# Token blocks of 128 at the joins of a two-layer model's linears, one unit a weight load, six split slots

## The chip, the cores and the metric

The kernel runs on one core of a Trainium2 chip. The metric is the device time of one execution in microseconds (us); lower is better.

## What is computed

256 tokens of width 1024 pass through two models of two layers each, all in float32. What matters here is the chain of linears and the norms between them:

```python
# first model, each layer
h = rms_norm(x, attn_norm_g);  proj = h @ w_in       # attention, pooling, gates
x = x + merged @ w_out                               # "out"
hf = rms_norm(x, ffn_norm_g)
u = depthwise_conv(hf @ ffn_w_up, ...)               # "ffn_up", 1024 -> 2 * 2816
x = x + (silu(u_gate) * u_val) @ ffn_w_down          # "ffn_down"
# second model, layer 0 (stick-breaking) and layer 1 (dilated attention)
h = h + rms_norm(mixer(rms_norm(h)) , g_mix_post)    # "sb_out" / "dil_out"
f = square(relu(rms_norm(h, g_ffn_pre) @ w_ff_in)) @ w_ff_out    # "ff_in", "ff_out"
h = h + rms_norm(f, g_ffn_post)
gate = sigmoid(rms_norm(h, g_ple) @ w_ple_gate)      # "ple_gate"
h = h + (p[i] @ w_ple) * gate                        # "ple_up", p[i] has width 256
```

## The kernel before

All engines run the same list of steps, made by `Plan`; each engine works off its own part of each step in that order, and semaphores join them. So the list sets each engine's queue, and a step that waits holds up what stands behind it on that engine.

Weights come in units of 128 x 1024 float32: `weight_units` cuts a linear's columns into panels of 512 (a panel's result fills one of four slots of PSUM, two banks each) and its rows into pairs of k tiles of 128. Two units make one load (`load`, line 752, `RAW_SLOTS` = 4 buffers of two units). A step `split` turns a unit into a rounded high part on ScalarE (line 1279) and the rest, the low part, on VectorE (line 1674), into one of `SPLIT_SLOTS` = 4 pairs of buffers; `prefetch(n)` puts the splits of units up to n + 3 ahead of unit n. A split waits until the products of the unit that held its slot are done (`w_used`). The activations too are held as high and low parts, with features on the partitions, and a product is three matmuls: high by high, high by low, low by high.

The step `mm` multiplies one unit with all 256 tokens. A linear named in `BY_FEATURE` (`ffn_up`, `ff_in` and others) puts out features on partitions: the weight tile of 128 x 128 is stationary and the 256 tokens move (lines 932, 934, 935); one unit has 2 k tiles x 4 feature tiles x 3 = 24 matmuls of 256 columns. Every other linear (`out`, `sb_out`, `dil_out`, `ff_out`, `ple_up`, `ple_gate`) puts out tokens on partitions: a tile of activations is stationary and 512 weight columns move (lines 941, 943, 945), 12 matmuls a unit, 6 for each block of 128 tokens.

Between two linears stands a norm, over both blocks of tokens at once. After `out`: residual add (line 1915), squares on ScalarE and VectorE (1299, 1693), the power on GpSimd (2174), the scaled x (`xn`: 1306, 1708), then `turn`: eight transposes for each half of the features on TensorE (895), high part on ScalarE (1289), low part on VectorE (1683), and the first unit of `ffn_up`. After `sb_out`, `dil_out` and `ff_out`: squares of the result (`y_square`, 1516), a step on VectorE (2001), the power on GpSimd (2183), `y_add` in three parts (2013, 2017), `turn` as above, and the first unit of `ff_in` or `ple_gate`. `ple_up` (two units) stands between `ff_out` and the turning for `ple_gate`; `post_norm_begin` issues the norm ahead of it and `post_norm_end` the turning behind it. The operand of `ple_up` is made by the step `emb` (four transposes, ScalarE 1533, VectorE 2037), issued between `ff_in` and `ff_out`, right behind `take_ff` of the last panel of `ff_in` (VectorE 2026, ScalarE 1525 and 1264, VectorE 2030).

In `dilated`, an iteration issues `dil_scores` n (TensorE 1170; mask and maximum on VectorE 2072; the exponential on ScalarE 1584), `dil_norm` n-1 (VectorE 2083, 2085), `dil_av` n-3 (TensorE 1206), and `dil_pturn` n-2 (transposes 895; copies on ScalarE 1593 and VectorE 2093). ScalarE's copies stand behind the exponential of the same iteration.

Of the kernel before, what the change touches and what calls it, by code (L numbers as in the profile page):

```python
# [39 lines left out]
SPLIT_SLOTS = 4  # L40
# [16 lines left out]
def weight_plan():  # L57
# [21 lines left out]
    for l in range(DEPTH):  # L79
# [18 lines left out]
def weight_units():  # L98

    units, loads, at = [], [], 0  # L100
    for name, layer, source, rows, panels in weight_plan():
# [10 lines left out]
        for i in range(0, len(own), 2):  # L112
            pair = own[i:i + 2]
            size = sum(u["w"] * u["nk"] for u in pair)
            inside = 0
            for u in pair:
                u["load"], u["inside"] = len(loads), inside
                inside += u["w"] * u["nk"]
            loads.append((at, size))
            at += P * size  # L120
# [32 lines left out]
def constants():  # L153
# [26 lines left out]
    for keys, q0 in ((P, 0), (SEQ, P)):  # L180
        for dil in DIL:
# [12 lines left out]

STAGE_MIX, STAGE_FFN = (0, 2), (1, 3)
# [6 lines left out]
         "dil_in": (0, 1, 2), "dil_out": (0, 1), "ff_in": (0, 1, 2, 3), "ff_out": (0, 1), "ple_up": (2, 3),  # L202
         "ple_gate": (0, 1)}
# [3 lines left out]
TURN_BANKS = {STAGE_FF[0]: (6, 7, 4, 5), STAGE_FF[1]: (4, 5, 6, 7), STAGE_PLE[0]: (4, 5, 6, 7),  # L207
              STAGE_PLE[1]: (4, 5, 6, 7)}
# [8 lines left out]
class Plan:  # L217


    def __init__(self):  # L220
# [3 lines left out]
        self.panel_end = {}  # L224
# [29 lines left out]
    def unit(self):  # L254
        self.prefetch(self.n_used)
        self.add("mm", self.n_used)
        self.n_used += 1
# [7 lines left out]
    def linear(self, name, l, take):  # L265
        while self.n_used < len(self.units):
            u = self.units[self.n_used]
            if (u["name"], u["layer"]) != (name, l):
                break
# [6 lines left out]
    def whole(self, name, l, take):  # L276
        for _ in self.linear(name, l, take):
            pass

    def half_done(self, g, half, scaled=False):  # L280
# [4 lines left out]
        def turn(pairs):  # L285
            for j in pairs:
                self.add("turn", g, j)

        def turn_and_square():
            turn((2 * half, 2 * half + 1))  # L290
            square()

        if scaled:
            square()
            if half:
                self.add("xn", g)
                turn((0, 1))
                self.after(AHEAD, lambda: turn((2, 3)))
        elif half:
# [4 lines left out]
    def residual(self, g, scaled=False):  # L304
        def take(panel):
            self.add("residual", g, panel)
            if panel:
                self.half_done(g, 1, scaled)
            else:
                self.after(2, lambda: self.half_done(g, 0, scaled))  # L310
        return take

    def post_norm(self, g):
        def take(panel):
            self.add("y_square", g, panel)
            if panel == 0:
                self.add("y_mean", g)
        return take

    def post_norm_begin(self, g):  # L320
        self.add("y_rstd", g)
        self.add("y_add", g, 0)
        self.add("y_add", g, 1)

    def post_norm_end(self, g):
        self.add("turn", g, 0)
        self.add("y_add", g, 2)
        self.add("turn", g, 1)
        self.add("square", g, 0)
        self.add("mean", g)  # L330

        def rest():
            self.add("turn", g, 2)
            self.add("turn", g, 3)
            self.add("square", g, 1)
            self.add("rstd", g)
        self.after(AHEAD, rest)

    def mixing(self, l):
# [79 lines left out]
        self.whole("out", l, self.residual(STAGE_FFN[l], True))  # L419

    def first_ffn(self, l):
        def take(panel):
            self.add("conv", l, panel)
            if panel % 2:
                self.after(1, lambda: self.add("ffn_mult", l, panel // 2))
                self.after(2, lambda: self.add("ffn_split", l, panel // 2))
        self.whole("ffn_up", l, take)
        self.whole("ffn_down", l, self.residual(STAGE_MIX[1] if l == 0 else STAGE_SB))

    def stick_breaking(self):  # L430
# [5 lines left out]
        product = self.linear("sb_out", 0, self.post_norm(STAGE_FF[0]))  # L436
# [16 lines left out]
        self.post_norm_begin(STAGE_FF[0])  # L453
        self.post_norm_end(STAGE_FF[0])

    def second_ffn(self, l):
        add = self.add
        add("load_ff", l)
        self.after(4, lambda: add("row", STAGE_FF[l]))
        self.whole("ff_in", l, lambda panel: add("take_ff", l, panel))  # L460
        add("emb", l)
        self.whole("ff_out", l, self.post_norm(STAGE_PLE[l]))
        self.post_norm_begin(STAGE_PLE[l])
        self.whole("ple_up", l, lambda panel: add("take_up", l, panel))
        self.post_norm_end(STAGE_PLE[l])
        self.after(4, lambda: add("keep", l))

        def take_gate(panel):
# [5 lines left out]
            else:  # L474
                self.after(2, lambda: self.half_done(STAGE_DIL, 0))
        self.whole("ple_gate", l, take_gate)

    def dilated(self):
# [18 lines left out]
        product = self.linear("dil_out", 0, self.post_norm(STAGE_FF[1]))  # L497

        n_units = DIL_H // 2 * TT
        for n in range(n_units + 3):  # L500
# [12 lines left out]
        for _ in product:  # L513
            pass
        self.post_norm_begin(STAGE_FF[1])
        self.post_norm_end(STAGE_FF[1])
# [50 lines left out]
class Kernel:  # L567
# [19 lines left out]
    def acc(self, name, panel):  # L587
        return self.slot[SLOTS[name][panel % len(SLOTS[name])]]
# [6 lines left out]
    def memory(self):  # L595
# [13 lines left out]
        self.raw = [sb(f"w_raw{i}", 2 * UNIT) for i in range(RAW_SLOTS)]  # L609
# [106 lines left out]
    def turn_bank(self, g, j):  # L716
        return TURN_BANKS.get(g, (4, 5, 4, 5))[j]

# [1617 lines left out]
```

## Time and profile before

| what | value |
|---|---|
| runs (3), median | 1570.98 us (1564.82 to 1572.13) |
| the profiled execution | 1568.98 us |
| its span | 1567.2 us |
| mean granted clock of TensorE | 0.987 |
| TensorE busy (matmuls) | 1502.9 us, 96% |
| VectorE, ScalarE, GpSimd busy | 1042.5, 828.8, 56.9 us |
| DMA queues' mean share | 44.3% and 0.7% |

The span is the time from the first to the last instruction of one traced execution. PE is TensorE's matmuls, PEld its weight loads, DVE VectorE, ACT ScalarE, POOL GpSimd. A granted clock of 1.00 is 2.4 GHz and 0.50 is 1.2 GHz. The duration of a matmul in a row includes its way through the array, so the pace is read from the starts of consecutive rows and not from their durations.

### The profile page before, as it was taken

To read this page: it belongs to the slowest core of one execution; us is meant where nothing else is said; L and a number is where in the kernel's file an instruction comes from. 1 tells how busy PE (TensorE), PEld (TensorE's weight loads), DVE (VectorE), ACT (ScalarE), POOL (GpSimd) and SP (SyncE) were. 2 spreads that over 40 slices of the span, in tenths; PEclk is the share of its full clock that TensorE was granted. 3 is DMA by queue.
4 is the path that set the end of the run, shared out by engine and by line. 5 is a ranking of instruction groups with operands and counts; after the bars stand their busy time and mean duration, and the time that the engine had idled before them with its cause. 6 is when DMAs were issued, how large, how long until landed. Compare 5 with 4: busy or idle time off the path is not lost.

```text
span 1567.2 us, 23619 instructions
## 1 busy us (share of the span) xinstructions
PE 1502.9 (96%) x9984; PEld 1360.2 (87%) x9984; DVE 1042.5 (67%) x1513; ACT 828.8 (53%) x1179; POOL 56.9 (4%) x58
## 2 busy tenths in 40 slices
PE   6999989999999999899999998999999998899997
PEld 5998979998899889899989977998878876899886
DVE  5798676786578877677856566665466557656446
ACT  4465545565456565465644564554455455555434
POOL 1110000000021000000000000000000000000000
PEclk9999999999999999999999999999999999999999
DMA  6433343455544334345555414545545540344551
GB/s 252 172 137 132 122 176 137 186 187 193 189 164 164 133 109 158 139 187 189 190 190 199 171 54 148 196 161 213 190 161 206 193 167 28 130 187 165 211 197 46
DMA packets 38298, 255.72 MB, mean 163 GB/s; under 512 B 4528, under 2 KB 5552, under 8 KB 8752
## 3 DMA queue, kind: packets, MB, share of 16 engines
q1 hardware_dynamic: 37904, 253.77, 44.3%
q8 instruction: 79, 1.29, 0.3%
q10 hardware_dynamic: 288, 0.43, 0.1%
q14 instruction: 27, 0.22, 0.0%
HBM read 253.14 MB, written 1.05 MB: 162 GB/s over the span
## 4 chain that ended last, share of the span: by engine, by line
PE 87%; DVE 6%; ACT 4%; issue 1%; POOL 1%; DMA 0%; ACTq 0%; DVEq 0%
PE psum L932 14%; PE psum L934 14%; PE psum L935 14%; PE psum L941 12%; PE psum L943 12%; PE psum L945 12%; PE psum L895 3%; PE psum L1045 1%; DVE w_low L1674 1%; PE psum L1075 1%; PE psum L1132 1%; ACT w_high L1279 1%; PE psum L1170 1%; POOL stat L2159 1%; DVE gates L1891 0%
## 5 line engine op out<-in xcount | busy, mean ns | idle before, releaser
L1674 DVE TENSOR_TENSOR w_low<-w_raw,w_high 128x1024 fp32r<-128x1024 f32 (+1 forms) x476 | 569.8, 1212 | 291.2 <-ACT w_high L1279 290.7
L1279 ACT ACTIVATE w_high<-w_raw 128x1024 fp32r<-128x1024 f32 (+1 forms) x476 | 495.9, 1051 | 364.2 <-PE psum L945 219.6
L932 PE MATMUL psum<-x_high,w_high 128*128 128x256 f32 x1600 | 459.6, 287 | 2.8 <-DVE x_low L1683 2.8
L934 PE MATMUL psum<-x_low,w_high 128*128 128x256 f32 x1600 | 454.7, 284 | 0.0
L935 PE MATMUL psum<-x_high,w_low 128*128 128x256 f32 x1600 | 454.4, 284 | 0.0
L932 PEld LDWEIGHTS psum<-x_high,w_high 128*128 128x128 f32 x1600 | 309.0, 193 | 9.1 <-issue 8.8
L934 PEld LDWEIGHTS psum<-x_low,w_high 128*128 128x128 f32 x1600 | 309.1, 193 | 0.2
L935 PEld LDWEIGHTS psum<-x_high,w_low 128*128 128x128 f32 x1600 | 309.0, 193 | 0.0
L941 PE MATMUL psum<-w_high,ff_high 128*128 128x512 f32 x256 | 99.8, 390 | 0.0
L945 PE MATMUL psum<-w_high,ff_low 128*128 128x512 f32 x256 | 99.6, 389 | 0.0
L943 PE MATMUL psum<-w_low,ff_high 128*128 128x512 f32 x256 | 99.6, 389 | 0.0
L932 PE MATMUL psum<-x_high_next,w_high 128*128 128x256 f32 x256 | 73.4, 287 | 0.4 <-DVE x_low_next L1683 0.4
L934 PE MATMUL psum<-x_low_next,w_high 128*128 128x256 f32 x256 | 73.1, 286 | 0.0
L935 PE MATMUL psum<-x_high_next,w_low 128*128 128x256 f32 x256 | 73.1, 285 | 0.0
L941 PE MATMUL psum<-w_high,x_high_next 128*128 128x512 f32 x176 | 69.2, 393 | 2.5 <-DVE x_low_next L1683 2.5
L941 PE MATMUL psum<-w_high,ffn_high 128*128 128x512 f32 x176 | 68.7, 390 | 0.0
L945 PE MATMUL psum<-w_high,x_low_next 128*128 128x512 f32 x176 | 68.5, 389 | 0.0
L943 PE MATMUL psum<-w_low,x_high_next 128*128 128x512 f32 x176 | 68.5, 389 | 0.0
L943 PE MATMUL psum<-w_low,ffn_high 128*128 128x512 f32 x176 | 68.5, 389 | 0.0
L945 PE MATMUL psum<-w_high,ffn_low 128*128 128x512 f32 x176 | 68.5, 389 | 0.0
L941 PE MATMUL psum<-w_high,x_high 128*128 128x512 f32 (+2 forms) x160 | 59.8, 374 | 7.2 <-DVE w_low L1674 4.7
L1448 ACT ACTIVATE scratch<-psum,cols 128x256 f32<-128x256 f32 x88 | 42.7, 564 | 35.1 <-PE psum L935 35.1
(249 smaller groups left out, 2364.1 us busy)
## 6 DMA issues: line engine op xcount, KB each, us to landing
w_raw<-in_weights SPq DMA_DIRECT2D x230, 1024.0 KB, 4.8
w_raw<-in_weights SPq DMA_DIRECT2D x4, 832.0 KB, 5.9
rows<-in_second_rows SPq DMA_DIRECT2D x4, 512.0 KB, 4.4
w_raw<-in_weights SPq DMA_DIRECT2D x2, 768.0 KB, 4.1
residual<-in_x SPq DMA_DIRECT2D x2, 512.0 KB, 6.6
w_raw<-in_weights SPq DMA_DIRECT2D x2, 512.0 KB, 3.3
out<-residual SPq DMA_DIRECT2D x2, 512.0 KB, 2.7
dil_masks<-in_consts SPq DMA_DIRECT2D x1, 576.0 KB, 5.7
```

What stands on the lines that cost most here:

```text
L895: return eng.transpose(out, src, ident)
L932: eng.matmul(o, wh[:, j, cut], high[:, k, :], start=k == 0 and f % 2 == 0, stop=False, skip_group_check=True)
L934: eng.matmul(o, wh[:, j, cut], low[:, k, :], start=False, stop=False, skip_group_check=True)
L935: d = eng.matmul(o, wl[:, j, cut], high[:, k, :], start=False, stop=end, skip_group_check=True)
L941: eng.matmul(o, high[:, k, cut], wh[:, j, :], start=k == 0, stop=False, skip_group_check=True)
L943: eng.matmul(o, high[:, k, cut], wl[:, j, :], start=False, stop=False, skip_group_check=True)
L945: d = eng.matmul(o, low[:, k, cut], wh[:, j, :], start=False, stop=end, skip_group_check=True)
L1045: d = eng.matmul(bank[4 + i][:, t * SEQ:(t + 1) * SEQ], qt[i][:, t * P:(t + 1) * P], kt[i], start=True, stop=True)
L1075: d = eng.matmul(bank[6][HD * i:HD * i + HD, 0:SEQ], val, m["probt"][i][:, kt * SEQ:(kt + 1) * SEQ], start=kt == 0, stop=kt == TT - 1, ski ...
L1279: act(self.unit_view(self.wh, u), raw, ACT.Copy).then_inc(sem("w_high"), 1)
L1448: d = act(o[:, f, :], acc[:, f, :], ACT.Identity, scale=conv_w[:, 2 * FT + ft:2 * FT + ft + 1], bias=conv_b[:, ft:ft + 1])
L1674: tt(self.unit_view(self.wl, u), raw, self.unit_view(self.wh, u), ALU.subtract).then_inc(sem("w_low"), 1)
```

## The change

The last four units of `out`, `sb_out`, `dil_out` and `ff_out`, and the first four of `ffn_up`, `ff_in` and `ple_gate`, are multiplied in two passes: all four with tokens 0 to 127, then all four with tokens 128 to 255. Norm, `y_add` and turning go by blocks of tokens too (`norm(t)`, `turn_t`: four transposes and four copies of 128 columns for each block and half of the features). Block 0's norm is issued behind the first pass of the last units and its turning within their second pass; block 1's norm behind that second pass and its turning within the first pass of the next linear. A feature-major linear then runs matmuls of 128 columns in those units. `w_used` counts a unit at its second pass. `ple_up` moves from behind `ff_out` to behind `emb`. Loads carry one unit, raw buffers hold one unit, split slots are six, and `prefetch` reaches five units ahead. ScalarE's exponential in the dilated attention becomes a step `dil_exp` behind `dil_pturn`.

```diff
-SPLIT_SLOTS = 4
+SPLIT_SLOTS = 6
 RAW_SLOTS = 4
...
         plan += [("ff_in", l, "w_ff_in_2", D, panels_of(0, D_FF_2)),
+                 ("ple_up", l, "w_ple_2", PLE, panels_of(0, D)),
                  ("ff_out", l, "w_ff_out_2", D_FF_2, panels_of(0, D)),
-                 ("ple_up", l, "w_ple_2", PLE, panels_of(0, D)),
                  ("ple_gate", l, "w_ple_gate_2", D, panels_of(0, D))]
...
-        for i in range(0, len(own), 2):
-            pair = own[i:i + 2]
-            size = sum(u["w"] * u["nk"] for u in pair)
...
+        for u in own:
+            size = u["w"] * u["nk"]
+            u["load"] = len(loads)
             loads.append((at, size))
...
+SKEWED = 4
...
-TURN_BANKS = {STAGE_FF[0]: (6, 7, 4, 5), STAGE_FF[1]: (4, 5, 6, 7), STAGE_PLE[0]: (4, 5, 6, 7),
-              STAGE_PLE[1]: (4, 5, 6, 7)}
+TURN_BANKS, TOKEN_BANKS = (4, 5, 4, 5), (6, 7, 6, 7)
...
+    def token_unit(self, n, t):
+        self.add("mm", n, t)
+        if t:
+            self.n_used = n
+            self.used()
...
+    def second_pass(self, units, between):
+        for i, n in enumerate(units):
+            self.prefetch(n)
+            self.token_unit(n, 1)
+            for step in between.get(i, ()):
+                self.add(*step)
+
+    def first_units(self, name, l, take, first, second):
+        units = self.own_units(name, l)[:SKEWED]
+        self.prefetch(units[0])
+        for i, n in enumerate(units):
+            self.token_unit(n, 0)
+            for step in first.get(i, ()):
+                self.add(*step)
+        self.second_pass(units, second)
+        self.panel_end[name, l, 0] = self.n_used
+        take(0)
...
+    def post_normed(self, g, name, l, units, into, take, extra):
+        add, panels = self.add, self.ended_panels(name, l, units)
+
+        def norm(t):
+            for p in panels:
+                add("y_square", g, t, p)
+                if p == 0:
+                    add("y_mean", g, t)
+            add("y_rstd", g, t)
+        norm(0)
+        add("y_add", g, 0, 0)
+        add("y_add", g, 0, 1)
+        self.second_pass(units, {1: (("turn_t", g, 0, 0),), 2: (("turn_t", g, 0, 1),)})
+        norm(1)
+        add("y_add", g, 1, 0)
+        add("y_add", g, 1, 1)
+        whole = (("turn_t", g, 1, 1), ("square", g, 0), ("mean", g), ("square", g, 1), ("rstd", g))
+        self.first_units(into, self.units[self.n_used]["layer"], take, {2: (("turn_t", g, 1, 0),), 3: whole}, {1: extra})
...
+        def norm(t):
+            add("residual_t", g, t)
+            add("square_t", g, t, 1)
+            add("rstd_t", g, t)
+            add("xn_t", g, t)
+        norm(0)
+        self.second_pass(units, {2: (("turn_t", g, 0, 0),), 3: (("turn_t", g, 0, 1),)})
+        norm(1)
...
+        self.first_units("ffn_up", l, take, {2: (("turn_t", g, 1, 0),), 3: (("turn_t", g, 1, 1),)}, {})
...
         self.whole("ff_in", l, lambda panel: add("take_ff", l, panel))
         add("emb", l)
-        self.whole("ff_out", l, self.post_norm(STAGE_PLE[l]))
-        self.post_norm_begin(STAGE_PLE[l])
         self.whole("ple_up", l, lambda panel: add("take_up", l, panel))
-        self.post_norm_end(STAGE_PLE[l])
-        self.after(4, lambda: add("keep", l))
+        self.whole("ff_out", l, self.y_panel(STAGE_PLE[l]), SKEWED)
...
+        self.post_normed(STAGE_PLE[l], "ff_out", l, self.first_pass("ff_out", l), "ple_gate", take_gate, (("keep", l),))
...
             if 2 <= n < n_units + 2:
                 add("dil_pturn", n - 2)
+            if n < n_units:
+                add("dil_exp", n)
+            if n == n_units:
+                self.prefetch(product[0])
             if n_units <= n < n_units + 2:
-                next(product)
+                self.token_unit(product[n - n_units], 0)
...
-        self.raw = [sb(f"w_raw{i}", 2 * UNIT) for i in range(RAW_SLOTS)]
+        self.raw = [sb(f"w_raw{i}", UNIT) for i in range(RAW_SLOTS)]
...
+                    if by_feature:
+                        c = slice(blocks[0] * P, (blocks[-1] + 1) * P)
                         for f in range(w // P):
                             cut = slice(f * P, (f + 1) * P)
...
+                            o = acc[:, f * SEQ:(f + 1) * SEQ][:, c]
+                            eng.matmul(o, wh[:, j, cut], high[:, k, c], start=k == 0 and f % 2 == 0 and blocks[0] == 0,
+                                       stop=False, skip_group_check=True)
+                            eng.matmul(o, wh[:, j, cut], low[:, k, c], start=False, stop=False, skip_group_check=True)
+                            d = eng.matmul(o, wl[:, j, cut], high[:, k, c], start=False, stop=end,
                                            skip_group_check=True)
...
-                d.then_inc(sem("w_used"), 1)
+                if blocks[-1]:
+                    d.then_inc(sem("w_used"), 1)
```

## Rows read from the trace of the kernel before

**Rows 1.** The profile page: busy time of the engines

```profile
PE 1502.9 (96%) x9984; PEld 1360.2 (87%) x9984; DVE 1042.5 (67%) x1513; ACT 828.8 (53%) x1179; POOL 56.9 (4%) x58
```

**Rows 2.** Timeline of TensorE, out into ffn_up, first layer, then second: start us, us, what

```profile
229.33 0.39 PE L945 MATMUL psum<-w_high,mixed_low 128*128 128x512 f32 x1
233.62 1.97 PE L895 MATMUL psum<-consts,scratch 128*128 128x128 f32 x8 [3.91 <-ACT scratch L1306]
236.67 0.55 PE L932 MATMUL psum<-x_high,w_high 128*128 128x256 f32 x1 [1.08 <-DVE x_low L1683]
...
637.53 0.39 PE L945 MATMUL psum<-w_high,mixed_low 128*128 128x512 f32 x1
...
644.41 0.55 PE L932 MATMUL psum<-x_high,w_high 128*128 128x256 f32 x1 [1.35 <-DVE x_low L1683]
```

**Rows 3.** Stretches behind the joins: busy time of five engines, granted clock, DMA share, GB/s

```profile
236.60:239.80 3.20, 3.13 (x15) 3.16 (x16) 2.00 (x3) 0.81 (x1) 0.00 (x0) 0.50 0.14 20
644.40:649.40 5.00, 4.99 (x23) 5.00 (x24) 1.87 (x3) 0.63 (x1) 0.00 (x0) 0.50 0.45 125
968.30:970.30 2.00, 2.00 (x9) 2.00 (x10) 1.97 (x4) 2.00 (x5) 0.00 (x0) 0.50 0.00 0
1345.90:1349.10 3.20, 3.20 (x15) 3.20 (x16) 3.17 (x7) 2.06 (x5) 0.00 (x0) 0.50 0.02 5
```

**Rows 4.** Timeline of TensorE, sb_out into ff_in, then dil_out into ff_in

```profile
960.80 0.39 PE L945 MATMUL psum<-w_high,sb_out_low 128*128 128x512 f32 x1
965.23 1.11 PE L895 MATMUL psum<-consts,residual 128*128 128x128 f32 x4 [4.04 <-DVE residual L2017]
...
968.27 0.55 PE L932 MATMUL psum<-x_high,w_high 128*128 128x256 f32 x1 [0.35 <-DVE x_low L1683]
...
1338.37 0.39 PE L945 MATMUL psum<-w_high,dil_out_low 128*128 128x512 f32 x1
...
1345.87 0.55 PE L932 MATMUL psum<-x_high_next,w_high 128*128 128x256 f32 x1 [0.35 <-DVE x_low_next L1683]
```

**Rows 5.** Timeline of TensorE, ple_up into ple_gate, first layer

```profile
1155.68 0.39 PE L945 MATMUL psum<-w_high,ple_low 128*128 128x512 f32 x1
1155.91 1.03 PE L895 MATMUL psum<-consts,residual 128*128 128x128 f32 x8
1159.39 0.47 PE L941 MATMUL psum<-w_high,x_high 128*128 128x512 f32 x1 [2.44 <-DVE x_low L1683]
```

**Rows 6.** Timeline of weight loads and matmuls of gates behind a pause

```profile
102.50 0.19 PEld L932 LDWEIGHTS psum<-x_high,w_high 128*128 128x128 f32 x1 [0.33 <-issue]
...
102.61 0.19 PEld L934 LDWEIGHTS psum<-x_low,w_high 128*128 128x128 f32 x1
...
102.84 0.28 PE L935 MATMUL psum<-x_high,w_low 128*128 128x256 f32 x1
...
102.96 0.28 PE L932 MATMUL psum<-x_high,w_high 128*128 128x256 f32 x1
```

**Rows 7.** Groups by line and form: out<-in xcount, busy us, mean ns

```profile
L895 PE MATMUL psum<-consts,ple_tokens 128*128 128x128 f32 x8 | 1.2, 272 | 0.0
```

**Rows 8.** The critical chain within the join sb_out into ff_in

```profile
961.23 1.28 ACT squares L1516 x4
...
962.77 0.71 POOL stat L2183
```

**Rows 9.** Timeline behind the transposes of emb, first layer: TensorE, VectorE

```profile
1063.32 0.48 PE L941 MATMUL psum<-w_high,ff_high 128*128 128x512 f32 x1
...
1067.75 0.75 DVE L2037 SCALAR_TENSOR_TENSOR ple_low<-psum,ple_high 128x256 fp32r<-128x256 f32 x2
```

**Rows 10.** Groups by line, dilated attention, 1287.4 to 1323.6 us: idle before, releaser

```profile
L1206 PE MATMUL psum<-scratch,dil_v 128*64 128x128 f32 x108 | 7.2, 277 | 3.8 <-ACT scratch L1593 3.8
```

**Rows 11.** The page: the low half of a split

```profile
L1674 DVE TENSOR_TENSOR w_low<-w_raw,w_high 128x1024 fp32r<-128x1024 f32 (+1 forms) x476 | 569.8, 1212 | 291.2 <-ACT w_high L1279 290.7
```

**Rows 12.** The critical chain of the first 10 us: start us, us, what

```profile
1.20 7.54 DMA consts<-in_consts
```

More of the change, by code:

```diff
@@ L263, in unit, with own_units, first_pass_done @@
             what()
-    def linear(self, name, l, take):
-        while self.n_used < len(self.units):
+    def own_units(self, name, l):
+        return [u["n"] for u in self.units if (u["name"], u["layer"]) == (name, l)]
+    def token_unit(self, n, t):
+        self.add("mm", n, t)
+        if t:
+            self.n_used = n
+            self.used()
+    def first_pass_done(self, n):
+        self.token_passes.append(n)
+    def second_pass(self, units, between):
[4 more added lines that the diff above has]
+                self.add(*step)
@@ L267, in linear @@
+    def linear(self, name, l, take, keep=0):
+        end = self.own_units(name, l)[-1] + 1 - keep
+        while self.n_used < end:
             u = self.units[self.n_used]
-            if (u["name"], u["layer"]) != (name, l):
-                break
             self.unit()
@@ L274, in linear, with whole, half_done @@
             yield
-    def whole(self, name, l, take):
-        for _ in self.linear(name, l, take):
+    def whole(self, name, l, take, keep=0):
+        for _ in self.linear(name, l, take, keep):
             pass
-    def half_done(self, g, half, scaled=False):
+    def half_done(self, g, half):
         def square():
@@ L283, in square @@
             self.add("rstd" if half else "mean", g)
-        def turn(pairs):
-            for j in pairs:
-                self.add("turn", g, j)
         def turn_and_square():
-            turn((2 * half, 2 * half + 1))
+            self.add("turn", g, 2 * half)
+            self.add("turn", g, 2 * half + 1)
             square()
[L293 to L299, printed above, removed]
+        if half:
             self.after(AHEAD, turn_and_square)
@@ L418, in mixing, with first_half @@
         self.whole("branch_mla", l, last_branch)
-        self.whole("out", l, self.residual(STAGE_FFN[l], True))
+        g = STAGE_FFN[l]
+        def first_half(panel):
+            add("residual", g, panel)
+            for t in range(TT):
+                add("square_t", g, t, 0)
+            add("mean", g)
+        self.whole("out", l, first_half, SKEWED)
+        units = self.first_pass("out", l)
+        self.ended_panels("out", l, units)
+        def norm(t):
[6 more added lines that the diff above has]
+        norm(1)
     def first_ffn(self, l):
@@ L435, in stick_breaking @@
         values = self.linear("sb_values", 0, lambda panel: add("take_v", panel))
-        product = self.linear("sb_out", 0, self.post_norm(STAGE_FF[0]))
+        product = self.linear("sb_out", 0, self.y_panel(STAGE_FF[0]), SKEWED)
         add("sb_table")
@@ L496, in dilated @@
         turn_late()
-        product = self.linear("dil_out", 0, self.post_norm(STAGE_FF[1]))
+        product = self.own_units("dil_out", 0)
         n_units = DIL_H // 2 * TT
@@ L1090, in tensor @@
             elif kind == "y_add":
-                g, part = key
-                if part:
-                    name = {STAGE_FF[0]: "sb_out", STAGE_FF[1]: "dil_out"}.get(g, "ff_out")
-                    s = SLOTS[name][part - 1]
-                    free[2 * s] = free[2 * s + 1] = (sem("y_added"), at(*step))
+                g, t, half = key
+                name, l = self.y_of(g)
+                free[2 * slot_of(name, l, half) + t] = (sem("y_added"), at(*step))
             elif kind == "emb":
```

298 lines of the change are left out of this document (175 added, 123 removed).

## The prediction

> **What bounds the kernel now.** I read the page first: TensorE is busy 1502.9 us, 96% of the span [rows 1], so all that better cover can win is its idle time and what a low clock adds to its products. The timeline of TensorE at the joins shows where part of that lies. In the first layer the last product of `out` starts at 229.33 and the first of `ffn_up` at 236.67, with eight transposes between; the second layer has 637.53 and 644.41 [rows 2]. `sb_out` into `ff_in` takes 960.80 to 968.27, `dil_out` into `ff_in` 1338.37 to 1345.87 [rows 4]; `ple_up` into `ple_gate` is mended already, it waits 2.44 us [rows 5]. Behind the four long joins the granted clock is 0.50 (1.2 GHz) for 3.2, 5.0, 2.0 and 3.2 us [rows 3]; TensorE had been idle for most of 7 us before.
>
> The other thing to read is the pace. A matmul of 256 columns starts 0.12 us after the last (102.84, 102.96) [rows 6], one of 512 columns 0.23 us (1155.68, 1155.91) [rows 5]. So 256 columns more cost 0.107 us, and 0.013 us are fixed.
>
> **The change, part by part.** I sum against the profiled execution, 1568.98 us (span 1567.2 and 1.8 around it), 2.0 below the median.
>
> 1. *Narrow matmuls (the largest term).* `ffn_up` and `ff_in` are feature-major: the token blocks split their moving operand. Four units at the start of each, twice two linears, are 16 units; 16 x 24 = 384 matmuls of 256 columns become 768 of 128, each with its own weight load. The token-major linears pay nothing: they only order their 12 matmuls a unit otherwise. The trace has no rounded matmul of 128 columns, so I bound it. From below: columns alone, 0.013 + 0.053 = 0.067 us. From above: plain float32, whose 128 columns are two passes; a transpose is one pass of that kind, eight take 1.03 us of which the last is 0.27 [rows 5, 7], so 0.109 us a pass, 0.218 for two. What lies nearest is the weight load: behind a pause, loads start at 102.50 and 102.61 [rows 6], 0.108 us apart, though the first matmul of 256 columns can't be done by then; a load occupies its path that long. With 256 columns it hides exactly behind the matmul, with 128 it can't. I take 0.112 us. Price: 768 x 0.112 - 384 x 0.12 = 86.0 - 46.1 = +39.9 us. (At 0.120 it is +46, at 0.067 +5.4, at 0.218 +121.)
>
> 2. *Joins after `out`.* Lost now: 7.34 less one product (0.23) and eight transposes (0.87) is 6.2 us, and half of 3.1 us of low clock, 1.5: 7.8. Second layer: 6.88 - 1.10 + 2.5 = 8.3. Afterwards the second pass, 4 x 6 x 0.227 = 5.4 us, covers block 0's norm (the old chain for both blocks took 233.62 - 229.56 = 4.1 us [rows 2]), but ScalarE and VectorE carry two splits of the second pass before they copy what was turned, each 1.21 us on VectorE [rows 11]. I estimate 1.9 us of waiting left at the first narrow product. Block 1's chain lies behind 4 x 24 x 0.112 = 10.8 us: covered. Gain 5.9 + 6.4 = -12.3.
>
> 3. *Joins into `ff_in`.* Lost now: 7.47 - 1.10 + 1.0 = 7.4 and 7.50 - 1.10 + 1.6 = 8.0 [rows 3, 4]. Block 0's transposes stand behind two half units, 2.7 us. From the last product's start to the transposes the old chain has 4.43 us [rows 4]; less 0.23 for that product, 0.64 for one block's squares (half of the 1.28 us of four rows) and an estimated 0.15 for fewer, longer instructions in `y_add` leaves 3.4 from the pass's end, a fifth of it the power on GpSimd [rows 8]: 0.7 us late. `dil_out` squares both panels of the block first: 1.3 late. Gain 6.7 + 6.7 = -13.4.
>
> 4. *`ff_out` into `ple_gate`*, twice. Lost now 2.45 each. Here the next linear is token-major, so block 1's chain (3.4 us, behind splits and block 0's copies on VectorE) has only 3 x 1.36 = 4.1 us of cover: I estimate 0.7 at block 0, 1.8 at block 1's transposes, 1.0 at its copies, 3.5 in all. +1.05 x 2 = +2.1.
>
> 5. *`ple_up` right behind `emb`.* Now the unit behind the transposes of `emb` is of `ff_out`, whose operand is ready: it starts at 1063.32. The low half of `emb` is finished only at 1067.75 + 0.75 = 1068.50 [rows 9], because on ScalarE and VectorE it stands behind the last `take_ff`. That order stays, and now `ple_up` waits for it, with everything behind it on TensorE: 5.15 us idle. A wait of 4 us was followed by a low clock at the long joins, so I add 1.5. +6.65 x 2 = +13.3. Ends: 0 only if TensorE had other work, which an in-order queue doesn't give it; 7.5 with 5 us of low clock.
>
> 6. *Dilated attention.* The copies of turned weights no longer stand behind an exponential; TensorE waits 3.8 us for them there [rows 10]. I take -3 (0 to -4): the exponential now starts later, but ahead of its norm there is the next unit's mask. The half units used as fill are shorter, which is in the 1.2 above within a microsecond.
>
> 7. *Loads of one unit, six slots.* Same bytes. TensorE starts when the constants land, 7.54 us after their issue [rows 12], in the queues' contention with the first weight loads, which now are half as long: -1 (0 to -3). Elsewhere splits are ready already; costed at nothing. The cover is that a load has four units' time, 11 us, to land. SyncE issues 476 loads for 238; nothing but loads stands behind them for long. `load_ff` waits for block 1's `y_add` and is issued behind two second-pass units of `ff_in`, later than that.
>
> Sum: 39.9 - 12.3 - 13.4 + 2.1 + 13.3 - 3 - 1 = +25.6, so 1594.6 for this execution; with the 2.0 to the median 1597.
>
> **Rivals.**
> - *A. Narrow matmuls are paced by their columns* (not slower). Place: the 16 units. For it: loads overlap matmuls in every row, and record lengths say nothing of occupancy. Against it: the two starts 0.108 us apart. Price 5.4 instead of 39.9; but 4 x 24 x 0.067 = 6.4 us cover block 1 worse, an estimated 2 us more waiting at each of the four joins, 8 in all. 1594.6 - 34.5 + 8 = 1568, median 1570. It decides below about 0.08 us a matmul.
>  The Trainium skill, "TensorE: Matmul & The Clock Gate", section "Back-to-back issue gap", has a sustained pace of about 81 ns for N=128 with a load each; by that the price would be 768 x 0.081 - 46.1 = +16, an estimate from its figure, and the time near 1578. The same page's "LDWEIGHTS" section gives a time per column that is 107 ns for 128 columns, and says the fast load is off for FP32 input; the two starts here (0.108 us) agree with that one.
> - *B. Below 256 columns the rounded format runs at plain float32's pace.* 0.218 us, +121, so 1597 + 81 = 1678. Nothing in the trace speaks for it but that nobody can see it there.
> - *C. The cover works fully.* Narrow matmuls as forecast, but no wait left at the joins (all 36.4 us of parts 2 to 4 gained, 12.8 more than the sum has), `emb` without a low clock (-3), the dilated attention and the start at their best (-3): 1597 - 19 = 1578.
>
> **Chances.** Forecast 0.66, A 0.15, B 0.10, C 0.09. A measurement of this kernel tells apart some 0.5%, 7.9 us: faster is below 1563.1, slower above 1578.8. The forecast's case runs from 1582 (best gains) to 1612 (0.120 us a matmul, 5 us of low clock after `emb`) and is nearly all slower (0.65 of 0.66); B is slower (0.10); C is half and half; A gives faster 0.06, same 0.08, slower 0.01. A rest for gains that I don't see moves 0.02 to faster. Faster 0.08, same 0.13, slower 0.79. Range: the forecast's own, down to A's 1568, up to 1614; B stays out.
>
> **What would show it.** Rows of 128x128 form on the feature-major lines with starts 0.11 apart (A: 0.07, B: 0.22). The joins after `out` and before `ff_in` with under 2 us between products, no stretch of clock 0.50 behind them. New: a wait of TensorE of 5 us for `ple_low` at each of two places, with 0.50 behind it. TensorE's busy time up by about 35 us, its idle time down by only some 10. I'm wrong if the narrow starts are near 0.07, or if `ple_up` starts within a microsecond of `emb`'s transposes.

## The result and the profile after

The kernel before takes 1568.4 us (median of 4 runs of this comparison), the changed one 1628.84 us (1627.43 to 1631.28): a ratio of 1.0382, 95% interval 1.0363 to 1.0402. It is slower, as forecast, but by 60 us, more than twice the 26 that the prediction's sum gave, and above its range, which ended at 1614.

The profiled execution took 1629.22 us. Its page, span and busy time of the engines, answers to [rows 1]:

```profile
span 1627.4 us, 24890 instructions
...
PE 1568.0 (96%) x10368; PEld 1424.8 (88%) x10368; DVE 1047.5 (64%) x1543; ACT 839.3 (52%) x1235; POOL 58.8 (4%) x68
```

TensorE's busy time is up by 65 us, its idle time down by under 5. TensorE's own waits (who, for whom, total, times, longest) show what is left and what is new, and a row of TensorE's timeline shows one of the new ones:

```profile
PE psum L1024 <- DVE ple_low L2171: 8.5, 2, 5.1
...
PE psum L973 <- DVE residual L2152: 4.5, 6, 1.1
...
PE psum L1079 <- DVE squares L1852: 3.1, 3, 1.2
...
PE psum L1015 <- DVE x_low L1823: 2.5, 2, 1.2
...
1007.80 0.92 PE L1079 MATMUL psum<-squares,consts 128*128 128x128 f32 x4 [1.19 <-DVE squares L1852]
```

The 8.5 us for `ple_low` (the low half of `emb`) are the wait that part 5 foresaw. The `residual` and `x_low` waits are what is left of the long joins, 1.2 us at most each. New and not foreseen are two waits of 1.2 us of line 1079, one in each `ff_in`: the step `row`, which spreads the norm's factor and stood far behind the norm before, now stands behind the second unit of the second pass and waits for it.

The narrow matmuls themselves, timeline of TensorE at the start of `ffn_up` in the second layer:

```profile
644.21 0.30 PE L1015 MATMUL psum<-x_high,w_high 128*128 128x128 f32 x1 [1.25 <-DVE x_low L1823]
...
644.46 0.28 PE L1018 MATMUL psum<-x_high,w_low 128*128 128x128 f32 x1
644.57 0.27 PE L1015 MATMUL psum<-x_high,w_high 128*128 128x128 f32 x1
644.68 0.27 PE L1017 MATMUL psum<-x_low,w_high 128*128 128x128 f32 x1
644.79 0.28 PE L1018 MATMUL psum<-x_high,w_low 128*128 128x128 f32 x1
```

They start 0.11 us apart. Over whole stretches at the full clock the mean is 0.112, the value that the prediction took. But look at the clock of such stretches: first layer's `ffn_up`, then second layer's (two rows), then two for `ff_in` of either layer, up to the wait for `row` and behind it (columns as in [rows 3]):

```profile
232.70:254.90 22.20, 22.18 (x200) 22.20 (x200) 10.43 (x20) 8.24 (x17) 0.56 (x1) 1.00 0.37 123
644.20:646.20 2.00, 1.99 (x18) 2.00 (x19) 2.00 (x6) 0.38 (x2) 0.00 (x0) 1.00 0.78 238
646.30:687.10 40.80, 40.80 (x194) 40.80 (x194) 9.20 (x17) 9.86 (x20) 0.56 (x1) 0.50 0.20 69
989.50:1006.40 16.90, 16.90 (x154) 16.90 (x152) 11.86 (x26) 7.33 (x18) 2.15 (x3) 1.00 0.51 169
1008.40:1018.40 10.00, 10.00 (x49) 10.00 (x49) 2.45 (x2) 2.39 (x3) 0.00 (x0) 0.50 0.37 130
1382.80:1399.60 16.80, 16.80 (x153) 16.80 (x152) 11.76 (x26) 7.94 (x20) 2.33 (x4) 1.00 0.52 169
1401.90:1411.90 10.00, 10.00 (x49) 10.00 (x49) 2.45 (x2) 2.39 (x3) 0.00 (x0) 0.50 0.34 114
```

In the first layer all 22 us of narrow matmuls run at 1.00 (2.4 GHz). In the second the clock is 1.00 for 2 us, then 0.50 (1.2 GHz) for 41 us, and 194 matmuls (8 transposes and, at the end, 13 wide ones among them) start in 40.8 us, 0.21 us each. In `ff_in` the first pass and half of the second ran at 1.00; the two units behind the wait for `row` start at 0.50. The stretches at 0.50 last 41, 13.7 and 13.7 us, and behind their first fraction of a microsecond TensorE is never idle in them: half is lost, 34 us. All three end 2 to 3 us after the first wide matmul.

The time by stage, from the start of a linear's first matmul to that of the next one's (us; worked out from the starts in either trace; a wait ahead of a linear counts for the one before it):

| stage | before | after | difference | forecast |
|---|---|---|---|---|
| start to `out`, first layer | 206.5 | 207.3 | +0.9 | -1 |
| `out` + `ffn_up`, first layer | 159.3 | 162.9 | +3.6 | +4.1 |
| `out` + `ffn_up`, second layer | 159.6 | 182.3 | +22.7 | +3.6 |
| `sb_out` + `ff_in` | 128.0 | 144.1 | +16.1 | +8.4 |
| `dil_out` + `ff_in` | 117.9 | 134.2 | +16.3 | +8.4 |
| `ff_out`, `ple_up`, `ple_gate`, first and second | 245.4 | 250.4 | +5.0 | +5.1 |
| `dil_in` and attention | 140.5 | 136.5 | -4.1 | -3 |

(Part 5's 6.65 us a layer are split here: the wait for `emb`, 5.15, falls in the stage of `ff_in`, and the low clock behind it, 1.5, in that of `ple_up`.) What the table leaves out differs by 0.3 us in sum. So the first layer's `out` and `ffn_up` came out as forecast; the same code in the second layer costs 19 us more, and each `ff_in` nearly 8.

### The profile page after: what moved, and what is told of

Same layout as the page of the kernel before. It is cut to its first block, busy times and chain, and to the rows that moved or that the text cites. A ratio compares the mean times of both kernels' runs of the same rounds, so it can differ in the third digit from the quotient of the medians.

```text
span 1627.4 us, 24890 instructions
## 1 busy us (share of the span) xinstructions
PE 1568.0 (96%) x10368; PEld 1424.8 (88%) x10368; DVE 1047.5 (64%) x1543; ACT 839.3 (52%) x1235; POOL 58.8 (4%) x68
## 3 DMA queue, kind: packets, MB, share of 16 engines
HBM read 253.14 MB, written 1.05 MB: 156 GB/s over the span
## 4 chain that ended last, share of the span: by engine, by line
PE 89%; DVE 6%; ACT 3%; issue 1%; DMA 1%; POOL 0%; ACTq 0%; DVEq 0%; POOLq 0%
PE psum L1015 16%; PE psum L1017 15%; PE psum L1018 15%; PE psum L1024 12%; PE psum L1028 11%; PE psum L1026 11%; PE psum L973 3%; DVE w_low L1785 1%; PE psum L1142 1%; PE psum L1172 1%; PE psum L1227 1%; ACT w_high L1374 1%; DVE dil_weights L2207 1%; DVE scratch L2149 0%; DVE residual L2152 0%
## 5 line engine op out<-in xcount | busy, mean ns | idle before, releaser
L1015 PE MATMUL psum<-x_high,w_high 128*128 128x256 f32 (+1 forms) x1696 | 494.3, 291 | 2.5 <-DVE x_low L1823 2.5
L1017 PE MATMUL psum<-x_low,w_high 128*128 128x256 f32 (+1 forms) x1696 | 489.7, 289 | 0.0
L1018 PE MATMUL psum<-x_high,w_low 128*128 128x256 f32 (+1 forms) x1696 | 489.5, 289 | 0.0
L1015 PEld LDWEIGHTS psum<-x_high,w_high 128*128 128x128 f32 x1696 | 336.8, 199 | 8.3 <-issue 7.7
L1017 PEld LDWEIGHTS psum<-x_low,w_high 128*128 128x128 f32 x1696 | 337.0, 199 | 0.2
L1018 PEld LDWEIGHTS psum<-x_high,w_low 128*128 128x128 f32 x1696 | 336.9, 199 | 0.0
L1015 PE MATMUL psum<-x_high_next,w_high 128*128 128x256 f32 (+1 forms) x288 | 83.8, 291 | 0.0
L1017 PE MATMUL psum<-x_low_next,w_high 128*128 128x256 f32 (+1 forms) x288 | 83.6, 290 | 0.0
L1018 PE MATMUL psum<-x_high_next,w_low 128*128 128x256 f32 (+1 forms) x288 | 83.6, 290 | 0.0
L1562 ACT ACTIVATE scratch<-psum,cols 128x256 f32<-128x256 f32 x88 | 42.7, 562 | 36.8 <-PE psum L1018 36.8
```

The lines of the kernel that those rows point to most:

```text
L1015: eng.matmul(o, wh[:, j, cut], high[:, k, c], start=k == 0 and f % 2 == 0 and blocks[0] == 0, stop=False, skip_group_check=True)
L1017: eng.matmul(o, wh[:, j, cut], low[:, k, c], start=False, stop=False, skip_group_check=True)
L1018: d = eng.matmul(o, wl[:, j, cut], high[:, k, c], start=False, stop=end, skip_group_check=True)
L1562: d = act(o[:, f, :], acc[:, f, :], ACT.Identity, scale=conv_w[:, 2 * FT + ft:2 * FT + ft + 1], bias=conv_b[:, ft:ft + 1])
```

## The experiments

Two theories of the excess. **P**: a pause in or ahead of narrow matmuls loses the clock, and the narrow stream then doesn't get it back. **N**: the narrow stream loses it by itself. A third, **C**: chance, with nothing to do with the narrow matmuls.

**Narrow matmuls far from a join, and right behind one.** Both on the kernel before, in `mm`, one of the first two lines each (the comment names the run); each matmul then takes the columns `c0` to `c1` of the tokens:

```diff
+                        narrow = u["name"] in ("ffn_up", "ff_in") and u["panel"] in (1, 2)   # narrow_mid
+                        narrow = u["name"] in ("ffn_up", "ff_in") and u["panel"] == 0        # narrow_first
+                        for c0, c1 in (((0, P), (P, SEQ)) if narrow else ((0, SEQ),)):
                             for f in range(w // P):
...
```

> The kernel before, with only the matmuls of panels 1 and 2 of ffn_up and ff_in split into 128 columns (8 units in each of four linears, 32 units, far behind any join). All theories: the matmuls start 0.112 us apart at full clock, so 32 x 24 x (0.224 - 0.120) = +80 us. Theory P (the narrow stream needs a pause to lose the clock; it only keeps a low clock low): no stretch of clock 0.50 inside these stretches, about 1568 + 80 = 1648 us. Theory N (the narrow stream loses the clock by itself): most of the four stretches of 21.5 us fall to 0.50 and take twice as long, up to 1734 us.

> The kernel before, with only the matmuls of panel 0 of ffn_up and ff_in split into 128 columns: 16 units, as many narrow matmuls as the changed kernel has, right behind the four pauses of 7 us, at which the clock is 0.50 already. Price at full clock +40 us. If narrow matmuls hold a low clock low as long as they last (theories P and N alike), each of the four stretches runs 21.5 us instead of 10.8 at 0.50, and the time is 1568 + 40 + 4 x (10.8 - 1.7) = 1644 us. Rival C (the clock comes back 3 to 5 us behind the pause whatever runs, as it did before; the 41 us in the changed kernel were a chance): 1608 us.

`narrow_mid` took 1649.03 us (one run), 78 above 1571.3. Its four narrow stretches (matmuls' busy time, clock, DMA share):

```profile
249.70:292.30 42.60, 42.60 (x384) 1.00 0.32 110
677.70:720.30 42.60, 42.60 (x385) 1.00 0.31 110
1020.30:1063.00 42.70, 42.70 (x385) 1.00 0.30 108
1419.00:1461.70 42.70, 42.70 (x385) 1.00 0.29 106
```

Four times 42.6 or 42.7 us of unbroken narrow matmuls at 1.00: N is wrong, and the price of a narrow unit, (1649.03 - 1571.3) / 32 = 2.4 us, is what the prediction had (2.5).

`narrow_first` took 1640.12 us (one run), 69 above. Its first join, then the second half of panel 0 of the first `ff_in`:

```profile
236.40:246.30 9.90, 9.90 (x47) 0.50 0.31 106
248.20:252.00 3.80, 3.80 (x30) 0.80 0.02 4
253.00:264.90 11.90, 11.90 (x109) 1.00 0.25 88
1007.80:1038.20 30.40, 30.40 (x145) 0.50 0.10 37
```

Every stretch starts at 0.50, as it did with wide matmuls, and stays there for 10 us and more instead of 2 to 5. In three of the four the clock came back 0.6 to 1.8 us behind the transposes in the middle of the panel, in the midst of narrow matmuls (0.80, then 1.00); in one it stayed away until 2 us after the next wide matmul, 47.8 us in one piece. So a low clock is held longer under narrow matmuls, but not always to their end; the forecast that it lasts exactly as long as they do was too strict, and C, 1608 us, is out.

**The pause at `row`.** The changed kernel with `row` two units later, behind the last narrow unit (the step's four matmuls in plain float32 move with its wait):

```diff
-        self.first_units(into, ..., take, {2: (("turn_t", g, 1, 0),), 3: whole}, {1: extra})
+        self.first_units(into, ..., take, {2: (("turn_t", g, 1, 0),), 3: whole}, {3: extra})
```

> The changed kernel, with load_ff and row (for ple_gate: keep) behind the fourth unit of the second pass instead of the second. Theory P: in ff_in the clock fell at the 1.2 us in which TensorE waited for the norm's row in the midst of narrow matmuls, and these held it low for 13.7 us. Without that pause the second pass stays at 0.112 us a matmul: 2 x (1.2 + 6.8) = 16 us less, 1613 us, and the 41 us at 0.50 in the second layer's ffn_up stay as they are. Rival (the narrow stream falls by itself after some time, wherever it is): the 0.50 stretches in ff_in stay, 1627 us.

1616.28 us (1614.37 to 1635.63, ratio to before 1.0316, 1.0268 to 1.0365). The first narrow matmul of `ffn_up` in either layer with its wait, then the stretches of `ffn_up` in both layers and of the second passes of `ff_in`:

```profile
231.36 0.30 PE L1015 MATMUL psum<-x_high,w_high 128*128 128x128 f32 x1 [1.25 <-DVE x_low L1823]
...
662.27 0.30 PE L1015 MATMUL psum<-x_high,w_high 128*128 128x128 f32 x1 [1.25 <-DVE x_low L1823]
...
251.60:271.90 20.30, 20.30 (x98) 0.50 0.22 69
662.30:684.40 22.10, 22.10 (x199) 1.00 0.40 124
998.50:1009.10 10.60, 10.60 (x97) 1.00 0.37 110
1385.90:1396.50 10.60, 10.60 (x97) 1.00 0.35 118
```

`ff_in` now runs at 1.00 throughout, and its two stages take 137.5 and 127.8 us, 6.6 and 6.4 less: `row` amid the narrow matmuls was what cost 13.7 us at 0.50. That it was its wait and not its own four matmuls isn't shown, since both moved; for the wait speaks that the transposes, plain float32 too, stand amid the narrow matmuls in every trace and the clock never fell at them.

The 41 us at 0.50 in `ffn_up` are there again, but in the first layer and not in the second. Both layers have the same pause of 1.25 us ahead of the first narrow matmul (TensorE waits for `x_low` behind splits), in this and in the changed kernel. Over the traces of the changed kernel, `row_later` and the two runs below that keep it (`emb_early`, `two_narrow`) it occurs eight times. In four the clock fell, 1.9 to 2.7 us behind it: in the second layer of the changed kernel and of `emb_early`, in the first of the other two. One of the four executions of `row_later` took 1635.63 us at a mean clock of 0.968, where the profiled one took 1615.1 at 0.982. By these means it spent some 46 us more at 0.50 (an estimate), as much as one more such stretch. So this pause can cost the clock and need not, and the same program differs from one execution to the next; what decides it was not varied here and stays open.

**The wait for `emb`.** The changed kernel with

```diff
-        self.whole("ff_in", l, lambda panel: add("take_ff", l, panel))
-        add("emb", l)
+        def take_ff(panel):
+            add("take_ff", l, panel)
+            if panel == 6:
+                self.after(2, lambda: add("emb", l))
+        self.whole("ff_in", l, take_ff)
```

and another bank for its transposes in the first layer (bank 0 for 4).

> The changed kernel, with emb issued two units into the last panel of ff_in, into a bank that is free by then, instead of behind take_ff of that panel. If ple_up waits for emb's low half behind take_ff, 3.5 and 5.1 us of waiting, 1.4 us ahead of the transposes and some 3 us of low clock go: 1629 - 13 = 1616 us, and ple_up starts within 0.5 us of the last product of ff_in. Rival (the wait moves: ple_up or ff_out then waits for take_ff or for its splits): under 3 us gained, 1626 us or more.

1611.15 us (1607.88 to 1613.97; ratio 1.0258, 1.0228 to 1.0288), 17.7 us less by the medians. TensorE's waits no longer hold `ple_low`. This is the wait that went, in the changed kernel's trace (last copies of `emb`, then `ple_up`):

```profile
1104.33 1.23 DVE L2164 TENSOR_TENSOR ff_low<-scratch,ff_high 128x1024 fp32r<-128x1024 f32 x1 [2.21 <-ACT ff_high L1359]
...
1105.47 0.75 DVE L2171 SCALAR_TENSOR_TENSOR ple_low<-psum,ple_high 128x256 fp32r<-128x256 f32 x2
...
1106.36 0.77 PE L1024 MATMUL psum<-w_high,ple_high 128*128 128x512 f32 x1 [3.47 <-DVE ple_low L2171]
```

`ple_up` waited for VectorE, which had `take_ff`'s low half ahead of `emb`'s. Between the two traces lie 15.2 us: both stages `ff_in` are 5.1 us shorter, the stages behind them 1.7 to 2.1, and 1.5 are in the first turning of the program, where no edit was made. So the edit gained nearly 14 us, as forecast (13); the rest of the 17.7 is not its own.

**Wide matmuls again, and half of them.** Two edits of the changed kernel in `first_units`, one each (the comment names the run):

```diff
+        if name in BY_FEATURE:                       # wide_first
+            for step in first.get(2, ()):
+                self.add(*step)
+            for i in range(SKEWED):
+                self.unit()
+                for step in (first.get(3, ()) if i == 0 else second.get(i, ())):
+                    self.add(*step)
...
+        if name in BY_FEATURE:                       # two_narrow
+            self.prefetch(units[0])
+            self.token_unit(units[0], 0)
+            self.token_unit(units[1], 0)
+            for step in first.get(2, ()):
+                self.add(*step)
+            self.second_pass(units[:2], {0: first.get(3, ()), 1: second.get(1, ())})
+            return
```

> The changed kernel, with the first four units of ffn_up and ff_in in one pass of 256 columns again, behind the turning of both blocks (second half of the features of block 1 behind the first unit). If the narrow matmuls and the clock that they hold low are the loss: 39.9 us of price and 20.5 + 2 x 6.8 us of low clock go, block 1's norm is uncovered again at four joins (about 5.5 us of idle and 1.5 of low clock each, 28 in all): 1629 - 40 - 34 + 28 = 1583 us. Rival (the low clock came with the new waits of 1.2 us, and not with the narrow matmuls): the long low stretches stay, 1617 us.

> The changed kernel, with two instead of four narrow units at the start of ffn_up and ff_in (the next two of the panel in one pass of 256 columns). Half of the price goes, 20 us, and the low clock has half as many matmuls to slow, some 17 us less; cover for block 1's norm falls from 10.8 to 5.4 us, of the 8.7 us that it takes with no cover at all, some 2 to 3 us of idle more at each of four joins, +10. 1629 - 20 - 17 + 10 = 1602 us. Rival (the cover is worth more than the price): 1629 us or more.

`wide_first`: 1608.19 us (1607.09 to 1609.01; ratio 1.0246, 1.0222 to 1.0269), 21 less than the changed kernel where 46 were expected. Its join after `out`:

```profile
230.04 0.60 PE L983 MATMUL psum<-consts,scratch 128*128 128x128 f32 x4
236.90 1.11 PE L983 MATMUL psum<-consts,scratch 128*128 128x128 f32 x4 [6.25 <-ACT scratch L1430]
240.50 0.55 PE L1025 MATMUL psum<-x_high,w_high 128*128 128x256 f32 x1 [2.48 <-DVE x_low L1833]
```

Without cover block 1's chain leaves TensorE idle for 6.25 + 2.48 us, more than the kernel before lost for both blocks (3.91 + 1.08, [rows 2]). My 5.5 us had forgotten what stands ahead of it on VectorE and ScalarE: in this trace, three splits that the second pass of the last units sets free at double rate, and block 0's copies. In `ff_in` `row` waits 3.6 us on top of that. The long stretch at 0.50 in the second layer's `ffn_up` is gone with the narrow matmuls (that stage takes 163.8 us, 18.6 less); in the first, which had the full clock, four narrow units or none made no difference (162.9 and 163.2 us).

`two_narrow`: 1620.03 us (1618.88 to 1621.66; ratio 1.0313, 1.0299 to 1.0327), not 1602. With two narrow units a pause of 2.4 us (`ffn_up`) or 2.9 (`ff_in`) falls in the midst of them, and every join has a low clock in the midst of narrow matmuls; the stretch at the first join, its part ahead of that pause, and the stretch in the first `ff_in`:

```profile
236.40:260.00 23.60, 21.21 (x101) 0.50 0.21 70
...
236.40:241.60 5.20, 5.20 (x27) 5.20 (x27) 1.87 (x3) 2.33 (x4) 0.56 (x1) 0.50 0.31 97
...
987.30:1007.60 20.30, 17.09 (x79) 0.50 0.35 104
```

In the second layer's `ffn_up` and in both `ff_in` the clock fell during the pause or up to 2 us behind it. In the first layer it had fallen before, at 236.4, behind the pause of 1.25 us. Cover by a narrow unit can't save more than its own first pass, 24 x 0.112 = 2.7 us, and a narrow unit costs 2.5, so halving it was worth little; with the clock that went at every join the gain was 9 us where 27 were expected. My estimate held that half as many matmuls would lose half as much to the clock.

**Loads and slots, and the dilated attention, alone**, both on the kernel before: the first with the diff's edits of `SPLIT_SLOTS`, the loads and the raw buffers; the second with `dil_exp` only.

> The kernel before, with loads of one unit, raw buffers of one unit and six split slots, and nothing else but a wait of VectorE's rotation on its own predecessor that the order needs. TensorE starts about 1.2 us earlier and loses that and 1 us more at the second half of the first turning, which stands behind six splits instead of four; elsewhere nothing: 1571 us, within 0.2% of before. Rival (smaller loads or deeper splitting matter in mid-kernel): over 5 us either way.

> The kernel before, with only the exponential of the dilated attention as a step of its own behind dil_pturn. The waits of dil_av for copied weights, 3.8 us, go nearly whole: the stage dil_in with the attention takes 136.5 instead of 140.5 us, the kernel 1567 instead of 1571 us, the fastest of all so far. Rival (the exponentials come too late and scores or norms wait instead): no change or slower.

`loads_only`: 1571.16 us against 1571.16 (ratio 0.9996, 0.9985 to 1.0008): nothing, as expected; the prediction had -1. TensorE begins 0.7 us earlier and waits 1.0 us for the second half of the first turning. `dil_only`: 1567.35 us (ratio 0.9981, 0.9971 to 0.9990), the one of these two parts that pays; the stage takes 136.5 us, 4.0 less. But only 1.4 of them are waits that went. Its line that answers to [rows 10], then the whole attention in three traces, of the kernel before, of `narrow_first`, whose attention is the same code, and of `dil_only`:

```profile
L1208 PE MATMUL psum<-scratch,dil_v 128*64 128x128 f32 x108 | 7.2, 277 | 2.4 <-DVE scratch L2095 2.4
...
1287.20:1323.60 36.40, 28.27 (x275) 22.14 (x273) 25.62 (x75) 21.79 (x48) 0.00 (x0) 0.91 0.05 18
...
1345.30:1379.00 33.70, 25.52 (x275) 20.61 (x274) 25.62 (x75) 21.77 (x48) 0.00 (x0) 1.00 0.05 20
...
1287.40:1319.70 32.30, 25.48 (x274) 20.57 (x274) 25.39 (x75) 21.88 (x48) 0.00 (x0) 1.00 0.05 22
```

In the first the clock is 0.91, two stretches of 3.4 us at 0.50. At the full clock the old code takes 33.7 us and the new 32.3, so `dil_exp` is worth 1.4 us; the rest of the 4 is clock, which also falls in some traces with `dil_exp` (6.8 us at 0.50 in that of `no_pause`). Whether `dil_exp` makes that rarer isn't shown.

**No such pause at a narrow matmul.** The changed kernel with the edits of `row_later` and `emb_early`, and after `out`

```diff
-        self.second_pass(units, {2: (("turn_t", g, 0, 0),), 3: (("turn_t", g, 0, 1),)})
+        self.second_pass(units, {1: (("turn_t", g, 0, 0),), 2: (("turn_t", g, 0, 1),)})
```

> The changed kernel with all three pauses taken out of or away from the narrow matmuls: row (and load_ff, keep) behind the fourth unit of the second pass; emb two units into the last panel of ff_in; and after out, block 0's turning one unit earlier, so that its copies are done when the first narrow matmul is due. Theory P: no narrow stretch runs at 0.50. 1629 less 16 (row), 20.5 + 1.2 (the 41 us at 0.50 and the pause of 1.2 us ahead of it, at one of the two layers), 17 (emb, as its own run measured) gives 1574 us; what is left above the kernel before is the narrow matmuls' full-clock price less what the joins gain. Rival (the low clock comes from the narrow stream alone, and shows at some place in any case): one 0.50 stretch of 20 us or more, 1595 us.

1580.39 us (1580.11 to 1580.89; ratio 1.0059, 1.0045 to 1.0073). All four starts of `ffn_up` and `ff_in`:

```profile
230.50:252.50 22.00, 22.00 (x200) 1.00 0.41 136
641.10:663.10 22.00, 22.00 (x200) 1.00 0.42 137
965.90:987.90 22.00, 22.00 (x200) 1.00 0.43 143
1347.10:1369.10 22.00, 22.00 (x200) 1.00 0.45 147
```

1.00 throughout, and a mean granted clock of 0.997 in all four executions. Waits of 0.4 us ahead of the transposes after `out` and `sb_out` are left, and one of 1.1 us ahead of those after `dil_out`, 4 us before the first narrow matmul, which cost nothing. Of the changed kernel's 60 us, 48 to 51 (by the times, or by the distance from the kernel before of each comparison) were pauses and what they did to the clock. The clock is higher than before (0.987), and yet the kernel is 9 us slower, 6 more than expected. What is left is the full-clock price of the narrow matmuls, 40 us, less what the joins gain. The stages show it: `out` + `ffn_up` of the first layer 162.1 us against 159.3, and the two with `ff_in` 132.3 and 122.6 against 128.0 and 117.9.

**Keeping the array at work instead.** `dil_only`, and in the waits at the four long joins

```diff
+        def fill(b, n):
+            acquire(b)
+            for _ in range(n):
+                eng.matmul(bank[b][:, 0:SEQ], ident, self.consts[:, 0:SEQ], start=True, stop=True,
+                           skip_group_check=True)
...
+                if g in STAGE_FFN + STAGE_FF and j == 0:
+                    fill(0 if g == STAGE_FF[0] else 6, 7)
...
+                if g in STAGE_FFN and j == 1:
+                    fill(6, 2)
```

> The kernel before with dil_exp, and TensorE multiplying constants into a free bank while it waits at the four joins after out, sb_out and dil_out (seven plain float32 matmuls of 256 columns, 3.0 us, ahead of the first transposes; two more behind those after out). No wait is shortened. If idleness of TensorE is what costs the clock there, the 6.8 us at 0.50 behind each of these joins go, of which 3.1, 5.0, 2.0 and 3.2 us lay on products: 1567.4 - 6.6 = 1561 us. Rival (the clock isn't lost by that idleness, or the filling is late): 1567 us or more.

1561.52 us (1559.48 to 1561.94; ratio 0.9936, 0.9923 to 0.9950), 0.6% faster than the kernel before and where the sum put it. By the traces of `dil_only` and this run the four stages gained 1.8, 2.2, 0.3 and 0.7 us, 5.0 of the 6.6 expected, so a part of the match is chance. The join after `out`, to be read beside [rows 2], and the clock at all four, beside [rows 3]:

```profile
228.87 3.19 PE L902 MATMUL psum<-consts 128*128 128x256 f32 x14
232.94 1.09 PE L897 MATMUL psum<-consts,scratch 128*128 128x128 f32 x8 [0.88 <-ACT scratch L1318]
...
235.53 0.36 PE L940 MATMUL psum<-x_high,w_high 128*128 128x256 f32 x1 [0.63 <-DVE x_low L1695]
```

```profile
228.90:239.00 10.10, 8.59 (x56) 1.00 0.20 62
636.20:647.00 10.80, 9.29 (x67) 1.00 0.23 72
960.20:970.00 9.80, 8.61 (x58) 0.83 0.30 88
1332.50:1343.00 10.50, 8.18 (x49) 0.84 0.17 44
```

The real work starts nearly as late as before (the last product to the first of `ffn_up` 6.9 us, with 7.3 before), but at the full clock after `out`. At the other two, which have no filling behind the transposes, 3.4 us at 0.50 are left of 6.8. That the missing filling is the reason was not tested.

## Why the prediction was wrong

- **Part 1, the narrow matmuls.** The price at full clock was right: 768 matmuls, 0.112 us, taken from two weight loads 0.108 us apart. The Trainium skill, "TensorE: Matmul & The Clock Gate", section "LDWEIGHTS (loading the stationary operand)", gives a load time by columns that comes to an estimated 107 ns for 128 of them, which the measured pace bears out; the 81 ns in its section "Back-to-back issue gap", which stood beside rival A, is not what this format does here. (What the prediction says of the fast load for FP32 input stands on that page too, but under "Weight-path perf modes — Fast Weight Load (FWL) and DoubleRow".)
- **The step that failed** is in the same part: it priced 768 matmuls at one clock. I had read the clock behind the old joins [rows 3], put it down to idleness of most of 7 us, and let it vanish with the long waits (parts 2 and 3), while I left waits of 1.9, 0.7 and 1.3 us in the sum without asking what clock the matmuls behind them would have. The runs show that a wait of 1.2 us ahead of or amid narrow matmuls can lose it, and that it then stays away for 14 to 41 us. That is the second layer's 19 us, and 6.6 and 6.4 in the two `ff_in`, which `row_later` gave back: 32 of the 35 that were missing.
- **Part 2** was right: +3.6 for the first `out` and `ffn_up` where +4.1 was forecast. 1.25 us of waiting were left for 1.9.
- **Part 3** was right in kind and too hopeful by a little: with `row` and `emb` out of the way (`no_pause`) the stages are 4.3 and 4.7 us above the kernel before, where 10.0 - 6.7 = 3.3 was forecast. It left out `row`, which was named nowhere and moved nearer to its norm with the first units: two waits of 1.2 us, and the clock behind them.
- **Part 4** forecast 3.5 us of waiting; 2.5 came (0.4, 1.1 and 1.1) for 2.45 before, so +0.1 for +1.05. The stages themselves grew by 2.7 and 2.3, but 2.1 and 1.7 of that went with `emb`'s wait.
- **Part 5** was right: 3.5 us (with 1.4 ahead of the transposes, which now wait for the last panel's bank) and 5.1 us for 5.15 each; with the low clock behind them 7.3 and 6.8 us a layer by the traces of `emb_early`, for 6.65.
- **Part 6**: -4.1 for -3, and the match is luck: the wait of 3.8 us that it meant to win fell to 2.4. The other 2.7 us came from the clock in the attention, which was low for 6.8 us in the trace before and never in this one; `narrow_first` had it full with the old code too.
- **Part 7**: the start gained 1.2 us as forecast and lost it in the next wait, 2.1 us for the turning behind six splits, which I had costed at nothing (0.5 us in the traces of `emb_early` and `no_pause`, where nothing there was edited).

Rivals B (0.218 us) and C (full cover) did not come. B's number appeared all the same, 0.214 us, for another reason: 0.107 at half the clock.

## What to carry to other kernels

Before splitting a moving operand for the sake of order, look at the load of the stationary one: here 0.11 us a matmul was the floor, so 128 columns cost nearly what 256 do (0.112 and 0.120 us), and cover made of such matmuls is paid for in full. Keep every wait, even of one microsecond, away from such a stream, and price what lies behind a wait at the lower clock. Where a wait can't be covered with useful work, filling it with idle products on constants cost nothing that the traces show and gained more than any reordering here (5.8 us between the medians of `dil_only` and `dil_fill`).

## What the hardware showed that was not expected

- The clock is not given back for a busy array as such: with TensorE's rows busy without a gap it stayed at 0.50 for 41 us over narrow matmuls (in `ffn_up`, in three kernels, twice in the second layer and once in the first) and for 47.8 us in `narrow_first`. In all of these it came back 2 to 3 us after wide matmuls had begun. In the midst of narrow ones it came back three times, each time right behind eight transposes.
- It is not lost by them either: 4 x 42.7 us at 1.00. The same pause of 1.25 us lost it in four cases and not in four others.
- Plain float32 products of constants held the clock at 1.00 through the two joins after `out`, where it was at 0.50 for 6.8 us in the traces of the kernel before and of `dil_only`.
